# Windowed attention in one core's transformer block: column scores replaced by transposed rows

## The chip, the cores and the metric

The kernel runs on one core of one Trainium2 chip. The metric is the device time of one execution in microseconds (us), the median of several runs. Matrix products run on TensorE (PE in the profile), elementwise work on VectorE (DVE), ScalarE (ACT) and GpSimd (POOL), and SyncE (SP) issues most of the transfers.

## The reference

One block of a hybrid model over 1024 latent and 256 context tokens, width 1024: a combined input projection, a bidirectional scan, windowed attention, merging and output projection, and routed experts. The change concerns attention for the latent queries, with 16 query heads, 4 key and value heads of width 64, blocks of 128 queries, a window of 128 to each side, all 256 context keys, and one sink logit per head in the softmax:

```python
def block(i):
    start = i * ATTN_BLOCK
    qb = lax.dynamic_slice_in_dim(qg, start, ATTN_BLOCK, axis=1)
    kb = lax.dynamic_slice_in_dim(kp, start, span, axis=1)
    ...
    s_loc = jnp.einsum("bqkrd,bskd->bkrqs", qb, kb).astype(jnp.float32)
    s_loc = jnp.where(valid, s_loc, -jnp.inf)
    s_ctx = jnp.einsum("bqkrd,bskd->bkrqs", qb, k_ctx).astype(jnp.float32)
    p = jax.nn.softmax(jnp.concatenate([s_loc, s_ctx, s_sink], -1), axis=-1).astype(v.dtype)
    o = (jnp.einsum("bkrqs,bskd->bqkrd", p[..., :span], vb)
         + jnp.einsum("bkrqs,bskd->bqkrd", p[..., span:-1], v_ctx))
```

All types are float32. The kernel splits queries and keys in a high and a low part for products in the faster fp32r type; the probabilities and values are multiplied in full float32.

## The kernel before

The kernel is a row of stages, each a `Block` in which every engine runs a program of its own and engines wait for each other on semaphores; a stage begins when all engines have left the one before. The order of work on an engine is the order in which the program is written. `scan_output_stage` comes ahead of `attention_stage`; while it runs, SP loads keys, queries and masks of attention into freed buffers (`Early.load`, called with the scan's unit u from 23 on, between the stores of `yT`). Behind it come `branch_stage` and the rest.

`attention_stage` goes over 8 blocks of 128 queries. For a block it scores twice. The row scores (`row_scores`, L1727 and L1728) have queries on the partitions and 640 keys in the columns: `q1` holds a query's high part in rows 0 to 63 and its low part in rows 64 to 127, `k1` the high part of the keys twice, and `k2` the low part of the keys. DVE adds a mask and takes the row maximum (`maximum`, L1839). The maxima of 16 heads, with the sink, are turned (`turn_top`), split in two parts and loaded as two more rows of `q2`, against which `k2` holds ones: so the column scores (`column_scores`, L1743 and L1744), with 128 keys on the partitions and 4 heads x 128 queries in the columns, come out less their maximum. There are 5 key tiles and 4 groups of heads to a block, 4 tiles in the first and last block, 152 tiles in all. DVE masks the two edge tiles (L1857), ACT takes the exponential into `prob` (L1793), and PE sums values with it (`sum_values`, L1755) into `c_ps`: the weights are 64 columns of values, a column of ones, whose row gives the sum of the probabilities, and what follows. ACT copies the sums to `cols` (L1800).

The inverse of the sums takes a way through DRAM: SP gathers the row of sums (L1677), DVE adds the sink's share and inverts (L1866), SP writes the inverses to `inv_rows` and reads them back spread over 64 partitions, DVE divides (L1871), and SP stores the block to `aF` (L1692). `HEADS_AT` lays the row scores and maxima of block m between the column tiles of block m - 1; those of block 0 run alone at the start:

```python
for T in range(LAST):
    column_scores(T)
    if T in TURNS_AT:
        turn_top(TURNS_AT[T])
    if T in HEADS_AT:
        row_scores(*HEADS_AT[T])
    ...
    if T >= LAG:
        sum_values(T - LAG)
```

At the stage's end ACT and DVE also scale the first two tiles of `yT` for the next stage (L1823, L1906), whose first work on PE are the transposes of L2162.

## Time and profile before

| | |
|---|---|
| median of 3 runs | 2686.13 us (2683.49 to 2687.87) |
| span of the profiled execution | 2681.0 us; its own time is not given |
| mean granted clock of PE in it | 0.943 |
| busy, whole span | PE 2448.7 us (91%), DVE 1710.4 (64%), ACT 1090.6 (41%), POOL 466.5 (17%) |
| attention stage | 1226.6 us to 1549.4 us of the span |

The profile is of one execution. Its span runs from the first to the last instruction. Busy times of an engine overlap those of the others; of PE, printed durations contain the pipeline behind a product, so that products that follow each other overlap. The granted clock is a share of 2.4 GHz: 1.00 is the upper level and 0.50, 1.2 GHz, the lower.

### The profile page before, as it was taken

To read this page: it belongs to the slowest core of one execution; us is meant where nothing else is said; L and a number is where in the kernel's file an instruction comes from. 1 tells how busy PE (TensorE), PEld (TensorE's weight loads), DVE (VectorE), ACT (ScalarE), POOL (GpSimd) and SP (SyncE) were. 2 spreads that over 40 slices of the span, in tenths; PEclk is the share of its full clock that TensorE was granted. 3 is DMA by queue.
4 is the path that set the end of the run, shared out by engine and by line. 5 is a ranking of instruction groups with operands and counts; after the bars stand their busy time and mean duration, and the time that the engine had idled before them with its cause. 6 is when DMAs were issued, how large, how long until landed. Compare 5 with 4: busy or idle time off the path is not lost. (4 is left out here: it accounts for less than half of the span.)

```text
span 2681.0 us, 32789 instructions
## 1 busy us (share of the span) xinstructions
PE 2448.7 (91%) x12804; PEld 1996.5 (74%) x12804; DVE 1710.4 (64%) x1828; ACT 1090.6 (41%) x1363; POOL 466.5 (17%) x378
## 2 busy tenths in 40 slices
PE   7899999999999997998999879998982999999993
PEld 2788888887798785666666579997761788888882
DVE  5555555544245764685665467664665799999996
ACT  3333332221131112452333444433331677777772
POOL 0000010021003423792000000001433011111112
PEclk8899999999999998896999979998985999999996
DMA  5222234776337867996335199987335799999994
GB/s 221 77 78 80 74 116 119 184 242 222 109 115 262 300 219 215 315 277 151 62 77 111 41 258 257 255 229 231 117 110 221 296 383 403 403 398 395 396 376 141
DMA packets 359955, 572.12 MB, mean 213 GB/s; under 512 B 24973, under 2 KB 269165, under 8 KB 336449
## 3 DMA queue, kind: packets, MB, share of 16 engines
q1 hardware_dynamic: 328226, 464.99, 52.1%
q0 software_dynamic: 23376, 97.36, 11.3%
q10 hardware_dynamic: 8216, 7.90, 1.2%
q8 instruction: 90, 1.47, 0.2%
q14 instruction: 47, 0.39, 0.0%
HBM read 460.19 MB, written 104.49 MB: 211 GB/s over the span
## 5 line engine op out<-in xcount | busy, mean ns | idle before, releaser
L2714 DVE TENSOR_TENSOR e_wlo<-e_w,e_whi 128x2048 fp32r<-128x2048 f32 x188 | 425.6, 2289 | 43.9 <-ACT e_whi L2663 42.6
L2663 ACT CAST e_whi<-e_w 128x2048 fp32r<-128x2048 f32 x192 | 365.3, 1909 | 125.3 <-PE e_gu L2840 84.1
L460 PE MATMUL f_lat<-h_hi,w_hi 128*128 128x512 f32 x800 | 253.9, 399 | 8.0 <-DVE w_lo L611 8.0
L460 PE MATMUL f_lat<-h_lo,w_hi 128*128 128x512 f32 x800 | 251.2, 395 | 0.0
L460 PE MATMUL f_lat<-h_hi,w_lo 128*128 128x512 f32 x800 | 251.1, 395 | 0.0
L2174 PE MATMUL b_acc<-b_hi,b_whi 128*128 128x256 f32 x768 | 219.0, 285 | 8.3 <-issue 8.3
L2174 PE MATMUL b_acc<-b_lo,b_whi 128*128 128x256 f32 x768 | 218.3, 284 | 0.0
L2174 PE MATMUL b_acc<-b_hi,b_wlo 128*128 128x256 f32 x768 | 218.3, 284 | 0.0
L611 DVE TENSOR_TENSOR w_lo<-w_raw,w_hi 128x1024 fp32r<-128x1024 f32 x50 | 61.2, 1225 | 171.7 <-ACT w_hi L530 171.7
L460 PEld LDWEIGHTS f_lat<-h_hi,w_hi 128*128 128x128 f32 x800 | 137.9, 189 | 38.2 <-DVE w_lo L611 8.6
L1839 DVE CUSTOM_DVE_ANT_0 a_a_ps<-a_a_ps,shared 128x640 f32<-128x640 f32 x128 | 106.5, 833 | 87.6 <-PE a_a_ps L1728 83.0
L460 PEld LDWEIGHTS f_lat<-h_hi,w_lo 128*128 128x128 f32 x800 | 140.1, 188 | 29.8
L460 PEld LDWEIGHTS f_lat<-h_lo,w_hi 128*128 128x128 f32 x800 | 140.0, 188 | 29.8
L1755 PE MATMUL a_c_ps<-a_prob,a_v 128*128 128x512 f32 x304 | 155.8, 595 | 0.0
L2174 PEld LDWEIGHTS b_acc<-b_hi,b_whi 128*128 128x128 f32 x768 | 148.5, 193 | 8.5 <-issue 8.5
L1793 ACT ACTIVATE a_prob<-a_b_ps 128x512 f32<-128x512 f32 x152 | 89.3, 597 | 154.7 <-DVE a_b_ps L1857 88.5
L2174 PEld LDWEIGHTS b_acc<-b_lo,b_whi 128*128 128x128 f32 x768 | 148.5, 193 | 0.0
L2174 PEld LDWEIGHTS b_acc<-b_hi,b_wlo 128*128 128x128 f32 x768 | 148.4, 193 | 0.0
L625 DVE SCALAR_TENSOR_TENSOR conv_acc<-conv_in,conv_tap_cols,conv_acc 128x1284 f32<-128x1284 f32 (+1 forms) x96 | 145.0, 1511 | 3.4
L2840 PE MATMUL e_gu<-e_whi,e_xhi 128*128 128x512 f32 x512 | 140.7, 397 | 3.9 <-DVE e_xlo L2718 2.4
L2840 PE MATMUL e_gu<-e_wlo,e_xhi 128*128 128x512 f32 x512 | 138.6, 393 | 0.0
L2840 PE MATMUL e_gu<-e_whi,e_xlo 128*128 128x512 f32 x512 | 138.6, 393 | 0.0
(374 smaller groups left out, 5434.5 us busy)
## 6 DMA issues: line engine op xcount, KB each, us to landing
e_w<-in_w_gate_up SPq DMA_DIRECT2D x128, 1024.0 KB, 10.8
e_w<-in_w_down SPq DMA_DIRECT2D x64, 1024.0 KB, 9.4
w_raw<-in_w_in SPq DMA_DIRECT2D x50, 512.0 KB, 4.0
t_space<-xbcT POOLq DMA_DIRECT2D x18, 1280.0 KB, 6.4
before<-t_space SPq DMA_DIRECT2D x16, 1024.0 KB, 4.5
shared<-before SPq DMA_DIRECT2D x64, 256.0 KB, 6.2
l_w<-in_w_ssd_br SPq DMA_DIRECT2D x20, 768.0 KB, 6.9
xbcT<-t_out POOLq DMA_DIRECT2D x20, 640.0 KB, 4.4
```

Of the source, the lines that this page charges most:

```text
L460: mm = nc.tensor.matmul(o, weights[:, b, k, :], part[:, k, a:a + n], start=(k == 0 and n_pass == 0), stop=(k == KT - 1 and n_pass == 2))
L611: nc.vector.tensor_tensor(wlo[:, b], w[:, b], whi[:, b].bitcast(F32), ALU.subtract).then_inc(w_free, 1)
L625: nc.vector.scalar_tensor_tensor(conv[:, b, a:W_OUT], padded[:, b, a + c:c + W_OUT], tap[:, b, c:c + 1], conv[:, b, a:W_OUT], ALU.mult, AL ...
L1755: nc.tensor.matmul(out, values(v, c, g), prob[:, T % PR], start=first, stop=last).then_inc(tiles_summed, 1)
L1793: nc.scalar.activation(prob[:, T % PR], b_ps[:, T % 2], ACT.Exp, scale=SCALE).then_inc(exps_made, 1)
L1839: V.tensor_tensor_reduce(a_ps[:, h % 2, A0:A0 + KEYS], a_ps[:, h % 2, A0:A0 + KEYS], mask[variant(m)], 1.0, NEG, ALU.add, ALU.max, top[:, ...
L2174: mm = nc.tensor.matmul(acc[:, b, int(k >= KY), 0:NW], weights[:, b, k, :], part[:, k, at:at + NW], start=(k in (0, KY) and n_pass == 0), ...
L2663: nc.scalar.copy(whi[:, slot % SPLIT], w[:, slot]).then_inc(w_hi, 1)
L2714: V.tensor_tensor(wlo[:, slot % SPLIT], w[:, slot], whi[:, slot % SPLIT].bitcast(F32), ALU.subtract).then_inc(w_split, 1)
L2840: mm = nc.tensor.matmul(gu[:, 512 * c:512 * c + 512], part[:, b, k, :], weights[:, slot % SPLIT, 512 * c:512 * c + 512], start=(k == 0 and ...
```

## The change

Attention scores once. For a pair of heads, PE makes the row scores; the low part of the keys now stands in both halves of `k2`, and the second products of an even and an odd head use rows 0 to 63 and 64 to 127 of the array. The queries lie with their high part in the lower rows for even heads and in the upper for odd ones, so that a block loads in four DMAs; four query buffers replace three pairs. DVE adds the mask and takes the maximum as before, but writes the masked scores to `rows` in SBUF. ACT takes the exponential there with the negative maximum as its bias, and sums the row in the same instruction. PE transposes the probabilities, four heads of a key tile into one tile of `t_ps`, and ACT and DVE copy them in turn to `prob`, which now lies in a part of `l_wo` that the scan uses for its outputs: so ACT and DVE wait at the start until all of `yT` is stored. The value sums of four heads are two matmuls, of 64 weight columns and 256 columns each, into partitions 0 to 63 and 64 to 127. The inverses stay on the chip: POOL multiplies the unit matrix by them, and a product with ones spreads them over the partitions (L1695); DVE multiplies the sums by that. The stores go by half blocks, in four DMAs each. `STEPS` sets the order by hand: a step is a pair of heads, with transposes three steps and value sums five steps behind. Masked keys outside the sequence are left out in blocks 0 and 7, which have 512 keys.

```diff
+        self.spare = flat[:, 2 * D_INNER:4 * D_INNER]
...
-        self.q1 = [queries(one + NK), queries(three), queries(three + 2 * NQ)]
-        self.q2 = [queries(two + NK), queries(three + NQ), queries(three + 3 * NQ)]
+        self.q = [queries(one + NK), queries(two + NK)] + [queries(three + j * NQ) for j in range(2)]
...
+    def load_query(self, eng, qkH, qkL, m):
+        at, j = KV_LAT0 + m * P, m % len(self.q)
+        for half in range(2):
+            for odd in range(2):
+                part = qkH if half == odd else qkL
+                src = part[0:QH * HD, :].rearrange("(h o d) t -> o d h t", o=2, d=HD)[odd, :, :, at:at + P]
+                eng.dma_start(self.q[j][half * HD:half * HD + HD, odd::2].bitcast(F32), src).then_inc(self.q_in[j], 16)
...
-            eng.dma_start(self.k2[HD:HD + 2].bitcast(F32).rearrange("p g t -> p (g t)"), s.flat[1:2, :].to_broadcast([2, KVH * KV_TOK])).then_inc(self.keys_in, 16)
+            self.load_key(eng, qkL, high, self.k2, self.keys_in)
         if u == 29:
-            self.load_query(eng, qkH, low, self.q2[0], 0)
-            self.blank(s, eng, 0)
+            self.load_query(eng, qkH, qkL, 1)
...
-    ORDER = (0, 2, 1, 4, 3)
...
+    RB, TB, VB = 10, 3, 8
...
+    STEPS, BATCHES, MAKER = [], [], []
+    for i in range(STEP_COUNT):
+        step = []
+        u = (i - 3) // 2
+        if 0 <= u < LCHUNK * KVH:
+            half = (FIRST[u + 1] - FIRST[u] + 1) // 2
+            step += [("keys", p) for p in (range(FIRST[u], FIRST[u] + half) if i % 2 else range(FIRST[u] + half, FIRST[u + 1]))]
+        MAKER += [j % 2 for j in range(len(step))]
+        if i >= 7 and i % 4 == 3:
+            step.append(("values", (i - 7) // 4))
+            MAKER.append(0)
+        STEPS.append(range(len(BATCHES), len(BATCHES) + len(step)))
+        BATCHES += step
...
-        prob = own(st, nc, "a_prob", [P, PR, PER_KV, P])
...
+        rows = own(st, nc, "a_rows", [P, RB, KEYS])
+        prob = later.spare.rearrange("p (b h q) -> p b h q", h=PER_KV, q=P)
+        cols = own(st, nc, "a_cols", [P, 2, 2, 2, P])
+        diagonal, ones = own(st, nc, "a_diagonal", [P, 2, PER_KV, P]), own(st, nc, "a_ones", [P, HD])
...
+                def scores(i):
+                    n, g, h = i // HALF, (i % HALF) // 2, (2 * i) % QH
+                    if h == 0:
+                        pe.wait_ge(q_in[n % len(q)], 64 * (n // len(q)) + 64)
+                    a, w = CTX + n * P + (P if n == 0 else 0), width(n) - CTX
+                    spans = ((slice(A0, A0 + CTX), slice(0, CTX)), (slice(A0 + CTX, A0 + CTX + w), slice(a, a + w)))
+                    for odd in range(2):
+                        if i:
+                            pe.wait_ge(maxed, 2 * i - 1 + odd)
+                        for out, keys in spans:
+                            nc.tensor.matmul(a_ps[:, odd, out], q[n % len(q)][:, h + odd], k1[:, g, keys], start=True, stop=False)
+                    for out, keys in spans:
+                        for odd in range(2):
+                            part = slice(HD * odd, HD * odd + HD)
+                            mm = nc.tensor.matmul(a_ps[:, odd, out], q[n % len(q)][part, h + odd], k2[part, g, keys], start=False, stop=True)
+                            if out.start != A0:
+                                mm.then_inc(scored, 1)
...
+                    if kind == "keys":
+                        u, a, _ = PARTS[p]
+                        pe.wait_ge(exps_made, PER_KV * u + PER_KV)
+                        for j in range(PER_KV):
+                            mm = nc.tensor.transpose(out[:, j], rows[:, (PER_KV * u + j) % RB, a:a + P], ident)
+                    else:
+                        pe.wait_ge(diagonal_made, 2 * p + 2)
+                        for a in range(2):
+                            mm = nc.tensor.matmul(out[HD * a:HD * a + HD], ones[:], diagonal[:, a], start=True, stop=True)
+                    mm.then_inc(turned, 1)
...
+                def sum_values(u):
+                    c, g = u // 2, u % KVH
+                    if c >= 1 and u % 2 == 0:
+                        pe.wait_ge(normed, c)
+                    for p in range(FIRST[u], FIRST[u + 1]):
+                        wait_moved(pe, AT[p])
+                        _, _, chunk = PARTS[p]
+                        chunk -= chunk > CCHUNK
+                        for a in range(2):
+                            mm = nc.tensor.matmul(o_ps[HD * a:HD * a + HD, u % 2], v[:, chunk, HD * g:HD * g + HD], prob[:, p % VB, 2 * a:2 * a + 2],
+                                                  start=p == FIRST[u], stop=p + 1 == FIRST[u + 1])
+                        mm.then_inc(valued, 1)
...
+                for i in range(STEP_COUNT):
+                    if i < PAIRS:
+                        scores(i)
+                    if i >= 5 and i % 2 == 1:
+                        if i == 5:
+                            pe.wait_ge(v_in, 32)
+                        sum_values((i - 5) // 2)
+                    for k in STEPS[i]:
+                        turn(k)
...
+                def exponential(h):
+                    w = width(h // QH)
+                    act.wait_ge(negated, h // 2 + 2)
+                    nc.scalar.activation(rows[:, h % RB, 0:w], rows[:, h % RB, 0:w], ACT.Exp, scale=SCALE, bias=negtop[:, h:h + 1],
+                                         accum_out=sums[:, h:h + 1]).then_inc(exps_made, 1)
...
+                for g in range(GROUPS):
+                    act.wait_ge(later.y_out[g], 16 * LCHUNK)
+                    act.sem_inc(act_carrier, 1)
...
+                    V.tensor_tensor_reduce(rows[:, h % RB, 0:w], a_ps[:, h % 2, A0:A0 + w], mask[variant(n)][:, 0:w], 1.0, NEG,
+                                           ALU.add, ALU.max, top[:, h:h + 1]).then_inc(maxed, 1)
...
+                    V.tensor_tensor(cols[:, c % 2], o_ps[:], cols[:, c % 2], ALU.mult).then_inc(normed, 1)
...
+                for i in range(STEP_COUNT):
+                    if i < PAIRS:
+                        maximum(2 * i)
+                        maximum(2 * i + 1)
+                        negate(i)
+                        if i % 4 == 3:
+                            sink_argument(i // 4)
+                    if i >= 5 and i % 4 == 1:
+                        invert((i - 5) // 4)
+                    if i >= 8 and i % 4 == 0:
+                        norm((i - 8) // 4)
+                    for k in STEPS[i]:
+                        if MAKER[k] == 1:
+                            move(k)
...
+                        share = inverse[:, HALF * c + PER_KV * a:HALF * c + PER_KV * a + PER_KV]
+                        nc.gpsimd.tensor_tensor(diagonal[:, a], ident.unsqueeze(1).to_broadcast([P, PER_KV, P]),
+                                                share.unsqueeze(2).to_broadcast([P, PER_KV, P]), ALU.mult).then_inc(diagonal_made, 1)
...
```

On PE, before, an inner block repeats these rows (`a_c_ps` value sums, `a_b_ps` column scores, `a_a_ps` row scores of one head); each row of a value sum is two records in the trace.

```order
L1755 MATMUL a_c_ps<-a_prob,a_v 128x512
L1743 MATMUL a_b_ps<-shared 128x512
L1744 MATMUL a_b_ps<-shared 128x512
L1727 MATMUL a_a_ps<-shared 128x256
L1728 MATMUL a_a_ps<-shared 128x256
L1727 MATMUL a_a_ps<-shared 128x384
L1728 MATMUL a_a_ps<-shared 128x384
```

On PE, in the change, an odd step with the spreading of inverses and the even step behind it, in an inner block (`a_o_ps` value sums, `a_t_ps` transposes and spread inverses):

```order
L1678 MATMUL a_a_ps<-shared 128x256 x2
L1678 MATMUL a_a_ps<-shared 128x384 x2
L1707 MATMUL a_o_ps<-l_wo,a_v 64x256 x10
L1691 MATMUL a_t_ps<-shared,a_rows 128x128 x12
L1695 MATMUL a_t_ps<-a_diagonal,a_ones 64x512 x2
L1674 MATMUL a_a_ps<-shared 128x256
L1674 MATMUL a_a_ps<-shared 128x384
L1674 MATMUL a_a_ps<-shared 128x256
L1674 MATMUL a_a_ps<-shared 128x384
L1678 MATMUL a_a_ps<-shared 128x256 x2
L1678 MATMUL a_a_ps<-shared 128x384 x2
L1691 MATMUL a_t_ps<-shared,a_rows 128x128 x8
```

The column scores have gone, and the value sums of a group, spread over five tiles before, stand in one piece ahead of twelve transposes.

On SP's queue, at the end of the scan stage, the rows of the change from unit 27 on:

```order
L1211 DMA shared<-qkL 64x4x1536
L1332 DMA yT<-l_wo 128x512
L1211 DMA shared<-qkL 64x4x1536
L1332 DMA yT<-l_wo 128x512
L1219 DMA shared<-qkH 64x8x128
L1219 DMA shared<-qkL 64x8x128 x2
L1219 DMA shared<-qkH 64x8x128
L1332 DMA yT<-l_wo 128x512
L1240 DMA shared<-const_masks 128x640
L1332 DMA yT<-l_wo 128x512
```

Before, the second load of `qkL` was one of 2x6144 constants, and the four loads of queries were one of 64x16x128 and one of 2x2048 constants.

## Rows read from the trace of the kernel before

**Rows 1.** Busy time by stretch, attention stage; columns named in the first row.
```profile
core 0: us, PE busy (x) PEld busy (x) DVE busy (x) ACT busy (x) POOL busy (x), PEclk, DMA share, GB/s
1226.00:1257.00 31.00, 26.82 (x86) 20.31 (x87) 18.32 (x43) 3.16 (x3) 0.00 (x0) 0.50 0.84 165
1257.00:1536.00 279.00, 271.31 (x1044) 180.46 (x1042) 156.61 (x328) 109.71 (x198) 4.27 (x6) 0.99 0.34 70
1536.00:1549.00 13.00, 0.00 (x0) 0.00 (x0) 6.12 (x12) 5.85 (x8) 0.00 (x0) 0.57 0.20 49
```

**Rows 2.** Order of time (start, duration, engine, line, operation, idle before), PE, first products.
```profile
1226.59 0.55 PE L1727 MATMUL a_a_ps<-shared 128*128 128x256 f32 x1 [8.87 <-DMA shared<-const_flat]
...
1549.44 0.45 PE L2162 MATMUL b_tp<-l_ident,l_wo 128*128 128x128 f32 x1 [13.69 <-PEq L1635]
```

**Rows 3.** Order of time, PE and DVE, a step within block 3.
```profile
1411.72 0.28 PE L1727 MATMUL a_a_ps<-shared 128*128 128x256 f32 x1
...
1411.84 0.28 PE L1728 MATMUL a_a_ps<-shared 66*128 66x256 f32 x1
...
1411.96 0.34 PE L1727 MATMUL a_a_ps<-shared 128*128 128x384 f32 x1
...
1412.14 0.34 PE L1728 MATMUL a_a_ps<-shared 66*128 66x384 f32 x1
...
1412.31 1.02 PE L1755 MATMUL a_c_ps<-a_prob,a_v 128*128 128x512 f32 x2
1412.69 0.83 DVE L1839 CUSTOM_DVE_ANT_0 a_a_ps<-a_a_ps,shared 128x640 f32<-128x640 f32 x1 [1.03 <-PE a_a_ps L1728]
...
1413.40 0.40 PE L1744 MATMUL a_b_ps<-shared 66*128 66x512 f32 x1
...
1413.44 0.14 DVE L1839 DVE_READ_ACCUMULATOR2_ANT a_top<- 128x1 f32 x1
1413.64 0.28 PE L1727 MATMUL a_a_ps<-shared 128*128 128x256 f32 x1
```

**Rows 4.** Order of time, SP's queue, the store of a block's sums.
```profile
1532.27 0.63 SPq L1692 DMA_DIRECT2D aF<-a_cols  x1
```

**Rows 5.** Order of time, PE, eight transposes in the projection stage.
```profile
109.77 1.04 PE L479 MATMUL f_tp<-squares,f_out 128*128 128x128 f32 x8
```

**Rows 6.** Groups by line, DVE and ACT: shapes, count, busy us, mean ns.
```profile
L1857 DVE TENSOR_TENSOR a_b_ps<-a_b_ps,shared 128x512 f32<-128x512 f32 x56 | 39.0, 696 | 27.6 <-PE a_b_ps L1744 27.6
...
L1800 ACT COPY a_cols<-a_c_ps 128x512 f32<-128x512 f32 x32 | 18.8, 586 | 21.8 <-PE a_c_ps L1755 21.7
...
L1009 ACT ACTIVATE t_space<-t_space 128x640 f32<-128x640 f32 x1 | 0.7, 738 | 0.0
...
L1823 ACT ACTIVATION_READ_ACCUMULATOR a_a_ps<-l_wo 128x1 f32 x2 | 0.4, 190 | 0.0
```

**Rows 7.** Busy time by stretch, scan stage; columns as in group 1.
```profile
1160.00:1180.00 20.00, 19.70 (x105) 13.79 (x103) 15.58 (x31) 11.44 (x40) 18.64 (x17) 1.00 0.88 300
1190.00:1226.00 36.00, 27.27 (x144) 19.03 (x142) 23.79 (x39) 16.07 (x58) 31.56 (x25) 0.92 1.04 240
```

**Rows 8.** Order of time, the scan's last store and the first maximum.
```profile
1221.91 0.32 SPq L1333 DMA_DIRECT2D yT<-l_wo  x1
...
1228.17 0.83 DVE L1839 CUSTOM_DVE_ANT_0 a_a_ps<-a_a_ps,shared 128x640 f32<-128x640 f32 x1 [6.36 <-PE a_a_ps L1728]
```

**Rows 9.** Order of time, ACT and DVE, the end of attention.
```profile
1536.27 1.89 ACT L1823 ACTIVATE a_a_ps<-l_wo 128x2048 f32<-128x2048 f32 x1
...
1538.29 1.28 ACT L1825 ACT_TABLE_LOAD   x1
1538.30 0.15 DVE L1900 TENSOR_SCALAR l_mean<-l_ssq 128x1 f32<-128x1 f32 x1 [6.12 <-ACT a_a_ps L1823]
...
1539.82 1.28 DVE L1906 TENSOR_SCALAR l_wo<-l_wo,l_root 128x2048 f32<-128x2048 f32 x1 [0.69 <-ACT l_root L1825]
...
1545.39 2.49 DVE L1871 TENSOR_TENSOR a_cols<-a_cols,a_inverse 64x512 f32<-64x512 f32 x4 [1.78 <-DMA a_inverse<-inv_rows]
```

More of the change, by code:

```diff
@@ L1574, in attention_stage, with tiles @@
-    FIRST = [TILES.index((n, 0, 0)) for n in range(LCHUNK)]
-    LAST = len(TILES)
-    ENDS = [T for T in range(LAST) if T + 1 == LAST or TILES[T + 1][1] != TILES[T][1]]
-    LAG = 3
-    PR, QB = 6, 3
-    A0 = 256
-    LEAD = 3
-    VW = HD + 2
-    INVERT, DIVIDE = 8, 12
+    STEP_COUNT = PAIRS + 4
+    def tiles(n):
+        first = 1 if n == 0 else 0
+        last = 2 if n == LCHUNK - 1 else 3
+        return [(P * t, t) for t in range(CCHUNK)] + [(CTX + P * (t - first), CCHUNK + n + t) for t in range(first, last)]
@@ new lines, in width @@
+    def width(n):
+        return P * len(tiles(n))
+    PARTS = [(u, a, v) for u in range(LCHUNK * KVH) for a, v in tiles(u // KVH)]
+    FIRST = [[p for p, part in enumerate(PARTS) if part[0] == u][0] for u in range(LCHUNK * KVH)] + [len(PARTS)]
+    STEPS, BATCHES, MAKER = [], [], []
[11 more added lines that the diff above has]
+        BATCHES += step
@@ L1583, in attention_stage @@
+    RANK = [MAKER[0:k + 1].count(MAKER[k]) for k in range(len(BATCHES))]
+    AT = [BATCHES.index(("keys", p)) for p in range(len(PARTS))]
     with ExitStack() as st:
-        ident, edge, mask, k1, k2, q1, q2 = early.ident, early.edge, early.mask, early.k1, early.k2, early.q1, early.q2
+        ident, mask, k1, k2, q = early.ident, early.mask, early.k1, early.k2, early.q
         sink, negsink = own(st, nc, "a_sink", [P, QH]), own(st, nc, "a_negsink", [P, QH])
-        v = own(st, nc, "a_v", [P, NV * KVH * VW + P - VW])
@@ L1625, in edges_before, with wait_moved @@
[L1625 to L1644 removed]
+        def wait_moved(eng, k):
+            eng.wait_ge(moved[MAKER[k]], RANK[k])
@@ L1714, in _ @@
+                for c in range(HALVES):
+                    store(c)
+                    m = len(q) + c // 2
+                    if c % 2 == 0 and m < LCHUNK:
+                        sp.wait_ge(scored, QH * (m - len(q) + 1))
+                        early.load_query(sp, qkH, qkL, m)
             @block.tensor
             def _(pe):
-                def row_scores(m, h):
-                    g, j, i = h // PER_KV, m % QB, QH * m + h
+                def scores(i):
+                    n, g, h = i // HALF, (i % HALF) // 2, (2 * i) % QH
@@ L1746, in sum_values @@
-                def sum_values(T):
-                    n, g, t = TILES[T]
-                    group = G * n + g
-                    first, last = T == 0 or T - 1 in ENDS, T in ENDS
-                    if first and group >= 2:
-                        pe.wait_ge(kept, group - 1)
-                    pe.wait_ge(exps_made, T + 1)
-                    c = t if t < CCHUNK else n + t
-                    out = c_ps[:, group % 2]
-                    nc.tensor.matmul(out, values(v, c, g), prob[:, T % PR], start=first, stop=last).then_inc(tiles_summed, 1)
+                        pe.wait_ge(q_in[n % len(q)], 64 * (n // len(q)) + 64)
@@ L1868, in divide @@
-                def divide(n, g):
-                    heads = slice(PER_KV * g, PER_KV * g + PER_KV)
-                    dve.wait_ge(inv_in, 16 * n + 16)
-                    V.tensor_tensor(cols[0:HD, n % 2, heads], cols[0:HD, n % 2, heads], inverse[:, heads], ALU.mult).then_inc(divided, 1)
-                dve.wait_ge(early.const_in, 48)
-                for h in range(QH):
-                    maximum(0, h)
-                dve.wait_ge(const_in, 32)
-                V.tensor_scalar(negsink[:], sink[:], -1.0 / SCALE, None, ALU.mult).then_inc(negated, 1)
@@ L1898, in inverse_mean @@
+                norm(HALVES - 1)
                 def inverse_mean(n):
@@ L2011, in _ @@
                 load_gates(0)
-                sp.wait_ge(later.a_out, 16 * LCHUNK)
+                for out in later.a_out:
+                    sp.wait_ge(out, 64 * LCHUNK)
                 load_piece(2)
```

376 lines of the change are left out of this document (117 added, 259 removed).

## Prediction

> **What bounds the kernel now.** I read the page first, then the busy time by stage, then the order of single instructions inside attention, and last the waits. The attention stage runs from PE's first score product at 1226.6 us to the first product of the next stage at 1549.4 [rows 1, 2]: 322.8 us. The reader should see three stretches in it [rows 1]. Up to 1257 the row scores and maxima of block 0 run alone, with PE at 26.82 busy of 31.00 us and a granted clock of 0.50, the lower level (1.2 GHz). From 1257 to 1536 PE is busy 271.31 of 279.00 us at 0.99, while DVE and ACT have 156.61 and 109.71: PE is the bound. From 1536 to 1549 PE has nothing: the last sums go through DRAM and back, and the next stage waits.
>
> In the middle stretch the starts tell what a product costs PE, as its printed durations overlap [rows 3]. One head of row scores starts products at 1411.72, 1411.84, 1411.96 and 1412.14 and the value sums at 1412.31: 0.12 us for 256 columns, 0.175 for 384, 0.59 a head. From the value sums to the next head it is 1.33 us; the two column score products take 0.235 each (1413.40 to 1413.64), which leaves 0.86 for a value tile. It is two records of 0.43 each in the trace. A block with five key tiles so costs PE 16 x 0.59 + 20 x (0.47 + 0.86) = 36.0 us.
>
> **What PE gives and takes.** The column scores go: 20 x 0.47 = 9.4 us a block, and with them the loading of maxima. The row scores stay. Added are 80 transposes a block; eight of them take 1.04 us, and without the 0.165 of pipeline behind the last (below) 0.11 each [rows 5], 8.8 us. The value tile becomes two matmuls of 256 columns, each with 64 columns of weights, into partitions 0 to 63 and 64 to 127. A pair of heads now has its second score products on rows 0 to 63 and 64 to 127 of the array. Whether such halves run side by side no row of this trace shows, since no two neighbouring products in it use separate parts of the array. The bounds are 0.43 and 0.86 us for a value tile, and 0.295 and 0.59 for the second products of a pair. The nearest row is the upper one. I still take the lower: the halves share no rows or columns of the array, no output partition and no wait, and each pair stands in a row on PE's queue. The products that spread the inverses (two of 512 columns, two halves of 0.43 each) take 1.29, as only the middle of four pieces overlaps; 1.72 without it.
>
> The Trainium skill ("TensorE: Matmul & The Clock Gate", Part 3) says that matmuls in distinct column groups run concurrently, with a measured 2.38x for three. The Trainium skill's "TensorEngine Tiling (Array Packing)", Key Properties, speaks against the change: switching the tiling mode drains TensorE. By the first page the sum is my 2647 below, where the upper row gives the 2740 of the first rival; by the second, the upper bound of the next part holds, 16 us more. No run here shows either yet.
>
> **What a change of shape costs.** A 384-column product is printed with 0.34 us and holds PE for 0.175 [rows 3], so emptying the array is worth at most 0.165; at least nothing. An inner block has 24 changes (5 in a pair of steps, 4 for the inverses): 0 to 4 us, and I take 2.
>
> **One step.** The new loop goes by pairs of heads, and PE's queue is: scores, in odd steps the value sums of a group of four heads, transposes. Scores have two buffers, and their second products end both, so PE and DVE take turns. From a last score product to its maximum it is 0.55 us (1412.14 to 1412.69), from one maximum to the next 0.89 (0.83 and 0.14 with an overlap), from a maximum's start to PE's next product 0.95 (1412.69 to 1413.64) [rows 3]. Even step: 0.55 + 0.89 + 0.95 = 2.39, then the second head's first products 0.295 and one of 0.12: the next last product starts after 2.81 us. Its eight transposes (0.88) lie in the wait. Odd step: 0.17 for the rest of the product, five value tiles 2.15, twelve transposes 1.32, four first products 0.59, and 0.12: 4.35, with the maxima (2.39) hidden. Four such pairs and two inverse products make an inner block 4 x 7.16 + 2.6 + 2 = 33.2 us. In blocks 0 and 7, with four tiles a head, it is 3.3 and 2.5: 4 x 5.8 + 2.6 + 2 = 27.8. Six and two: 254.8 us.
>
> The others fit below that. DVE in an inner block: 16 x 0.89, eight copies out of PSUM (a masked add over the same 128x512 tile takes 0.70 [rows 6]) 5.6, two norms 1.4, and small ones 2.5: 23.7. ACT: sixteen exponentials of 640 columns, 0.74 by the row of that width and 0.19 for the sum [rows 6], and fourteen copies of 0.59 [rows 6]: 23.1. POOL has four products a block, and two steps' time for each two. Were PE half as long, DVE's 23.7 would be the floor.
>
> **Ends.** The first steps have no transposes or sums (-4 us). The last pair's exponentials, transposes, copies and sums run bare: two maxima 1.5, ACT 1.9, sixteen transposes 1.8, copy and wait 0.9, values 1.7, the inverse 1.3 and the norm 0.7, about 10. The clock: PE is idle for 8.9 us before the stage [rows 2] and more now, so it starts at 1.2 GHz. A pair of steps then has about 12 us of PE work for 7.2. The stay there is between none and the 31 us of [rows 1]: 0 to 12 us, and I take 7. From first maximum to last sum: 254.8 - 4 + 10 + 7 = 268.
>
> The start: DVE and ACT now wait until the last yT store has landed, since prob lies in its buffer. SP's queue holds 1.5 MB more ahead of it for the second half of k2, 0.5 for block 1's queries, 0.2 less of masks and edges. The DMA engines are full there at 240 GB/s (1.04 of their time) [rows 7], so the store lands up to 8 us later, and the first maximum starts at 1236.2 instead of 1228.2 [rows 8]; bounds 0 and 12. Stores of a half block are now four DMAs, 64 issues at 0.63 us [rows 4], 40 us of SP's time, hidden.
>
> The tail: PE's 13.7 us wait [rows 2] held the sums' way through DRAM and two squares of 1.9 us [rows 9]. The squares now run beside the last sums. Left are six small instructions of 0.15 to 0.20 us for means and roots, the root's table 1.28, two scalings of 1.28, and the way into the next stage, 1.5 from the end of the last divide (1545.39 and 2.49) to 1549.4 [rows 2, 9]: with hand-overs 6.5.
>
> **The sum.** 1236.2 + 268 + 6.5 = 1510.7, against 1549.4: 38.7 us less. The stages behind it do what they did. The profiled span is 2681.0; its own time is not given, but the median of the three runs, 2686.1, lies 5.1 above, and I count these 5 us as what lies around the span. 2681.0 - 38.7 + 5.1 = **2647 us**.
>
> The bounds of this case: change of shape 0 or 4 a block (-16, +16), clock (-7, +5), start (-8, +4), and the second score products one behind the other (+0.29 in each of 64 steps, +19). Not all at once: **2620 to 2675**.
>
> **The rivals.**
> *The halves of the array don't run side by side*: the change then doesn't do what it says. A value tile stays at 0.86, an odd step is 6.80 and an even one 3.10. An inner block is 4 x 9.9 + 3.4 + 2 = 45.0, an edge block 37.5; with ends of 16 (my 13, and longer last sums) they make 361, and 1236.2 + 361 + 6.5 = 1603.7, 54 more: **2740**. This is the other side; it decides from about 0.68 us a value tile, where the 38.7 are used up (152 tiles x 0.25). For it: no row shows an overlap. Against it: the waits allow it. Chance 0.20.
> *The clock falls in the even steps.* PE idles there twice for about 0.6 us and is otherwise on transposes. For it: from 1226 to 1257 PE was 87% busy and stayed at 0.50 [rows 1]. Against it: in the scan stage before, with short products, it is 98.5% busy and stays at 1.00 [rows 7], and the wait after which the clock was low was longer, 8.9 us [rows 2]. If half the steps run at 1.2 GHz, a block gains 10 us: +80, **2727**. Chance 0.08. "TensorE: Matmul & The Clock Gate", Part 4 of the Trainium skill, says that the full clock doesn't engage for transposes, since they don't count as busy in the same way. By it this rival and its 2727 would be likelier; the transposes at 0.11 us of [rows 5] stand between long products and don't settle it.
> *Values overlap, but the turn-taking costs more*: late copies into three PSUM tiles or late exponentials hold PE, 0.3 us a step and the score halves in a row: +19 + 19, **2685**, no change. Chance 0.06; where only half of it comes, it is about 2666 and within my case.
> My own case has 0.66.
>
> **Chances and range.** A change of 0.2% (5 us) is about what this kernel's runs can tell from none. Faster 0.69 (my case and half of the third rival), within 0.2% 0.03 (its other half), slower 0.28 (the first two). The range reaches from my case's low end to the first rival with little beyond: 2618 to 2742.
>
> **What would show it.** In the profile after: a value tile's two halves at starts that make 0.43 a tile (0.86 is the first rival); even steps near 2.8 us and odd ones near 4.4 from last score product to last; transposes 0.11 apart; granted clock 1.00 after the first 20 us; first maximum near 1236; the next stage's first transposes near 1511, 6 to 7 us after the last value sum. I am wrong if the stage is longer than 323 us, or if DVE, not PE, has no idle time in it.

## The result, and the profile after

| | before | after |
|---|---|---|
| median, same chip | 2686.73 us (4 runs, 2683.49 to 2687.87) | 2637.26 us (4 runs, 2633.18 to 2639.67) |
| ratio | | 0.982, 95% interval 0.980 to 0.983 |
| span of the profiled execution | 2681.0 us | 2637.1 us |
| attention, PE's first product to the next stage's | 322.8 us | 268.3 us |

The change makes the kernel 49 us faster; 2647 had been forecast, with 2620 to 2675 for the likeliest case. In the profile the gain is 44 us. Three marks split it: the scan's last product on DVE, the first maximum, and the first product of the next stage.

Order of time of the kernel after, DVE and PE (start, duration, engine, line, operation, shapes, idle before):

```profile
1226.58 0.69 DVE L1514 TENSOR_TENSOR l_wo<-l_w,l_wo 128x512 f32<-128x512 f32 x1
...
1236.31 1.19 PE L1674 MATMUL a_a_ps<-shared 128*128 128x256 f32 x4 [13.14 <-POOL a_ones L1846]
...
1241.83 0.18 DVE L1807 TENSOR_SCALAR a_negsink<-a_sink 128x16 f32<-128x16 f32 x1 [14.56 <-DMA a_sink<-in_attn_sink]
1242.56 0.69 DVE L1775 CUSTOM_DVE_ANT_0 a_rows<-a_a_ps,shared 128x512 f32<-128x512 f32 x1 [0.55 <-DVE a_negsink L1807]
...
1500.11 0.69 DVE L1800 TENSOR_TENSOR a_cols<-a_o_ps,a_cols 128x512 f32<-128x512 f32 x1 [3.60 <-ACT a_cols L1739]
...
1504.58 3.40 PE L2098 MATMUL b_tp<-l_ident,l_wo 128*128 128x128 f32 x16 [5.13 <-PEq L1635]
```

The same product that ends the scan, before the change:

```profile
1221.12 0.69 DVE L1515 TENSOR_TENSOR l_wo<-l_w,l_wo 128x512 f32<-128x512 f32 x1
```

From the scan's last product to the first maximum it was 7.05 us (1221.12 to 1228.17 [rows 8]) and is 15.98. From the first maximum to the next stage it was 321.3 us ([rows 2, 8]) and is 262.0. So the change gives 59.3 us and takes 8.9 at the start: 50.4 net, where the medians differ by 49.5. The profile shows less because its scan, whose arithmetic is the same, ended 5.5 us later than in the execution of before, and the stages behind took 1 us more. In the twelve further profiles below this product starts anywhere from 1219.6 to 1228.2 us, so nothing about attention is read from it; all intervals below start behind it.

Busy time by stretch, after (columns as in [rows 1]):

```profile
1226.00:1242.00 16.00, 1.92 (x8) 1.43 (x8) 1.41 (x3) 0.00 (x0) 0.15 (x2) 0.55 1.08 255
1242.50:1258.00 15.50, 13.10 (x66) 10.08 (x68) 9.68 (x31) 8.77 (x23) 0.00 (x0) 0.60 1.05 180
1258.00:1499.00 241.00, 234.76 (x1722) 157.76 (x1718) 154.13 (x417) 157.38 (x355) 36.74 (x38) 1.00 0.23 51
```

PE still bounds the stage (234.76 of 241 us), DVE and ACT have 154 and 157, and the clock is at its upper level but for the part up to 1258 (0.55 and 0.60 in the first two rows). The reader should see that "busy" is too kind here: PE's printed products contain their pipeline, and the steps show idle time that this row does not.

Order of time, PE, two steps inside block 3:

```profile
1364.55 0.56 PE L1678 MATMUL a_a_ps<-shared 64*128 64x256 f32 x4
...
1365.04 1.09 PE L1691 MATMUL a_t_ps<-shared,a_rows 128*128 128x128 f32 x8
...
1366.03 0.56 PE L1674 MATMUL a_a_ps<-shared 128*128 128x256 f32 x2
...
1366.77 0.56 PE L1674 MATMUL a_a_ps<-shared 128*128 128x256 f32 x2 [0.18 <-DVE a_top L1775]
...
1367.26 0.56 PE L1678 MATMUL a_a_ps<-shared 64*128 64x256 f32 x4
...
1367.75 2.38 PE L1707 MATMUL a_o_ps<-l_wo,a_v 128*64 128x256 f32 x20
...
1370.07 1.53 PE L1691 MATMUL a_t_ps<-shared,a_rows 128*128 128x128 f32 x12
...
1371.35 0.83 PE L1674 MATMUL a_a_ps<-shared 128*128 128x256 f32 x4
...
1372.11 0.56 PE L1678 MATMUL a_a_ps<-shared 64*128 64x256 f32 x4
```

Five value tiles take 2.32 us from start to start, 0.464 each, against 0.86 before ([rows 3]): the halves run side by side. The single records of this row tell it more closely. Each of the ten products is two records; the two halves' records start 0.007 us apart, and the next two 0.216 behind them. So a tile inside the row costs 0.432 us, and the remaining 0.16 of the 2.32 stand at its two ends, where the shape of the products changes. Twelve transposes take 1.28. The four second products, worth 0.295 us of columns, hold PE for 0.49. In the even step (1364.55 to 1367.26, 2.71 us) the first head's first products start at 1366.03 and are worth 0.295, yet the second head's start at 1366.77, when its maximum has freed the buffer: 0.44 us without work. The odd step (1367.26 to 1372.11) is 4.85 us and has none.

### The profile page after: what moved, and what is told of

It reads as the page before. It is cut to its first block and busy times, and to the rows that moved or that the text cites. A ratio compares the mean times of both kernels' runs of the same rounds, so it can differ in the third digit from the quotient of the medians.

```text
span 2637.1 us, 34496 instructions
## 1 busy us (share of the span) xinstructions
PE 2404.6 (91%) x13468; PEld 1967.1 (75%) x13468; DVE 1696.2 (64%) x1900; ACT 1140.2 (43%) x1538; POOL 497.9 (19%) x410
## 5 line engine op out<-in xcount | busy, mean ns | idle before, releaser
L2845 POOL DMA_INDIRECT moe<-e_y,e_token x15 | 42.2, 2811 | 498.3 <-DVE e_y L2671 468.0
L1775 DVE CUSTOM_DVE_ANT_0 a_rows<-a_a_ps,shared 128x640 f32<-128x640 f32 (+1 forms) x128 | 96.0, 788 | 48.2 <-PE a_a_ps L1678 47.6
L1729 ACT ACTIVATE a_rows<-a_rows,a_negtop 128x640 f32<-128x640 f32 (+1 forms) x128 | 101.6, 796 | 31.1 <-DVE a_negtop L1781 31.0
```

The source lines that it names most:

```text
L1729: nc.scalar.activation(rows[:, h % RB, 0:w], rows[:, h % RB, 0:w], ACT.Exp, scale=SCALE, bias=negtop[:, h:h + 1], accum_out=sums[:, h:h + ...
L1775: V.tensor_tensor_reduce(rows[:, h % RB, 0:w], a_ps[:, h % 2, A0:A0 + w], mask[variant(n)][:, 0:w], 1.0, NEG, ALU.add, ALU.max, top[:, h:h ...
L2845: pool.indirect_dma_start(moe, bass.IndirectOffsetOnAxis(ap=token[:, e:e + 1], axis=0), y[:, e % 2], None, compute_op=ALU.add).then_inc(y_ ...
```

## The experiments

Each kernel is the change with one edit, or an earlier one of these with one more. They ran on several chips, each beside runs of the kernel before on its own chip, whose medians go from 2683.8 to 2687.2: the ratios, not the medians, compare kernels of different chips. Beside medians I use two intervals of each profile: A, from the scan's last product to the first maximum, and B, from the first maximum to the start of DVE's last multiplication of the sums. Kernels with the same start differ in A by 1 us (e4 and e7 by 1.7), and kernels with the same steps in B by 0.3, so B tells far more than a median, whose runs spread over 3 to 11 us.

| kernel | median us | ratio to before (95%) | A us | B us |
|---|---|---|---|---|
| the change | 2637.3 | 0.982 (0.980 to 0.983) | 16.0 | 257.6 |
| e1 value halves apart | 2678.7 | 0.996 (0.994 to 0.997) | 17.0 | 297.2 |
| e2 full rows | 2635.9 | 0.981 (0.979 to 0.983) | 16.3 | 257.2 |
| e3 by head | 2615.0 | 0.973 (0.972 to 0.975) | 16.5 | 237.6 |
| e4 start | 2629.6 | 0.979 (0.977 to 0.980) | 11.4 | 257.4 |
| e5 by head, 64 rows | 2666.7 | 0.993 (0.990 to 0.996) | 16.3 | 285.2 |
| e6 double transposes | 2681.5 | 0.999 (0.998 to 1.000) | 16.4 | 304.3 |
| e7 = e3 + e4 | 2611.7 | 0.973 (0.971 to 0.976) | 9.7 | 237.4 |
| e8 = e7, later waits | 2609.4 | 0.972 (0.970 to 0.975) | 7.6 | 237.5 |
| e9 = e8, shorter tail | 2607.0 | 0.971 (0.969 to 0.972) | 7.8 | 237.0 |
| e10 = e9, sums split | 2615.5 | 0.973 (0.972 to 0.975) | 7.8 | 244.1 |
| e11 sums split alone | 2620.3 | 0.975 (0.973 to 0.977) | 16.4 | 243.1 |
| e12 = e9, stores shared | 2606.4 | 0.970 (0.968 to 0.971) | 7.5 | 237.1 |

### Do the halves run side by side?

**e1.** The loops over tiles and halves change places.

```diff
-                    for p in range(FIRST[u], FIRST[u + 1]):
...
-                        for a in range(2):
+                    for a in range(2):
+                        for p in range(FIRST[u], FIRST[u + 1]):
...
```

> Same products in another order: the five products into partitions 0 to 63 first, then the five into 64 to 127, so that neighbours use the same columns of the array. Theory A (the halves of a value tile run side by side and PE bounds the odd steps): a tile goes from the 0.464 us read after the change (five in 2.32) towards 0.86; with the one overlap left between the two rows of five that is 4 x 0.4 = 1.6 to 1.9 us a group, 32 groups, +51 to +61 us: 2688 to 2698. Theory B (the gain came from the dropped column scores and the way through DRAM, and an odd step has slack or the overlap is not what makes the tile short): under +15 us, 2637 to 2652, and the value sums still take about 2.3 us a group.

Order of time, PE, e1:

```profile
1365.60 3.72 PE L1707 MATMUL a_o_ps<-l_wo,a_v 128*64 128x256 f32 x20
...
1369.25 0.98 PE L1691 MATMUL a_t_ps<-shared,a_rows 128*128 128x128 f32 x7
```

The same ten products take 3.65 us instead of 2.32, B grows by 39.6 us and the median by 41: theory A in kind, less in size. The reason is in the records. Below are stretches of 0.43 us within the value sums, PE busy and PEld busy as in [rows 1], where x counts the records in progress. The first is of the change; the other two are of e1, early in its row and in its middle:

```profile
1368.71:1369.14 0.43, 0.43 (x8) 0.29 (x6) 1.00 0.54 118
```

```profile
1366.48:1366.91 0.43, 0.43 (x3) 0.27 (x2) 1.00 0.36 81
1367.34:1367.77 0.43, 0.43 (x7) 0.33 (x4) 1.00 0.71 151
```

In e1 the ten records of one half go at 0.216 us a record, so a tile one half after the other costs 0.86 us, as before the change. But the other half's records begin 0.64 us before the first half's last one starts, and all 24 groups of five tiles look alike: there the halves overlap again. I had allowed for one overlapping product of 0.43. With none, e1 would be longer by 0.75 us in each of 32 groups and the loss about 64 us, an estimate from these starts (152 tiles of 0.43 are 65). So side by side is worth 0.43 us a tile, and without it the change's gain is gone.

### What is a change of shape worth?

**e2.** The second products use all rows:

```diff
-                            mm = nc.tensor.matmul(a_ps[:, odd, out], q[n % len(q)][part, h + odd], k2[part, g, keys], start=False, stop=True)
+                            mm = nc.tensor.matmul(a_ps[:, odd, out], q[n % len(q)][:, h + odd], k2[:, g, keys], start=False, stop=True)
```

> The second score products use all 128 rows (the low part of the keys lies in both halves, so this adds the product of the low parts) and can't run side by side; the array keeps one shape from scores to transposes. Theory A (side by side is worth 0.295 us a step and a change of shape next to nothing): +0.295 x 64 = +19 us, 2656. Theory B (the four second products take 0.49 us of which only 0.295 is columns, so a change of shape costs about 0.2 us, and with a second one before the transposes the packing of rows earns nothing): 0.59 for 0.49, and about 0.1 less in the transposes: -3 to +6 us, 2634 to 2643.

**e3** does the same and finishes each head before the next:

```diff
                         for out, keys in spans:
                             nc.tensor.matmul(a_ps[:, odd, out], q[n % len(q)][:, h + odd], k1[:, g, keys], start=True, stop=False)
-                    for out, keys in spans:
-                        for odd in range(2):
...
+                        for out, keys in spans:
+                            mm = nc.tensor.matmul(a_ps[:, odd, out], q[n % len(q)][:, h + odd], k2[:, g, keys], start=False, stop=True)
+                        mm.then_inc(scored, 1)
```

> As the full-row kernel, but each head is finished before the next one starts, so that its maximum can begin about 0.5 us earlier. Theory A (the 0.44 us that PE waits in each even step is turn-taking with DVE over two score buffers): that wait shrinks by 0.3 to 0.44 us in 32 even steps, 10 to 14 us less than the full-row kernel, about 2628. Theory B (DVE's and ACT's own work, or the copies, set the even step): the same as the full-row kernel within 3 us.

**e5** is e3 with the second products on `part`, the 64 rows of the change.

> Head by head as in the third run, but with the second products on 64 rows, as in the change: nothing runs side by side, and the products go 128, 64, 128, 64 rows in every step. Against the third run (2615) only the shape changes, four in a step where there were none. Theory A (a change of shape empties the array; the full-row kernel showed 0.49 for columns worth 0.295 on the way in and about 0.09 less in the transposes behind, so about 0.3 us for in and out): +0.5 us in each of 64 steps on a PE without idle time, +25 to +37 us, 2640 to 2652. Theory B (a change of shape costs nothing by itself): 2612 to 2618.

e2 costs nothing against the change (B 257.2 and 257.6): theory B. In the change the second products of a pair do start together, 0.003 us apart, so the overlap is there and something else takes its worth. PE in e2, the same two kinds of rows:

```profile
1364.10 0.83 PE L1674 MATMUL a_a_ps<-shared 128*128 128x256 f32 x4
1364.77 0.75 PE L1677 MATMUL a_a_ps<-shared 128*128 128x256 f32 x4
1365.37 0.38 PE L1690 MATMUL a_t_ps<-shared,a_rows 128*128 128x128 f32 x2
```

First and second products take 0.67 and 0.60 here, 1.27; in the change 0.76 and 0.50 (1371.35 to 1372.11 to 1372.61), 1.26. Products that overlap in pairs but change the shape twice cost what products in a row cost that don't. (Behind the scores of an odd step stand value sums, whose shape is another in both kernels. So e2 drops three changes in a pair of steps, 0.57 us at the price below, for 0.59 us of columns.)

e5 against e3 tells the price itself, since nothing runs side by side in either. PE in e5, then in e3, one step of scores each:

```profile
1368.97 0.54 PE L1674 MATMUL a_a_ps<-shared 128*128 128x256 f32 x2
1369.44 0.56 PE L1677 MATMUL a_a_ps<-shared 64*128 64x256 f32 x2
1369.93 0.56 PE L1674 MATMUL a_a_ps<-shared 128*128 128x256 f32 x2
1370.42 0.55 PE L1677 MATMUL a_a_ps<-shared 64*128 64x256 f32 x2
1370.90 1.09 PE L1689 MATMUL a_t_ps<-shared,a_rows 128*128 128x128 f32 x8
```

```profile
1369.59 0.54 PE L1674 MATMUL a_a_ps<-shared 128*128 128x256 f32 x2
1369.96 0.46 PE L1676 MATMUL a_a_ps<-shared 128*128 128x256 f32 x2
1370.26 0.45 PE L1674 MATMUL a_a_ps<-shared 128*128 128x256 f32 x2
1370.55 0.46 PE L1676 MATMUL a_a_ps<-shared 128*128 128x256 f32 x2
1370.85 1.03 PE L1688 MATMUL a_t_ps<-shared,a_rows 128*128 128x128 f32 x8
```

Each pair of products takes 0.49 us with a change of shape behind it and 0.295 without: 0.19 to 0.20 us a change. B grows by 47.6 us. Four changes in an even step and three in an odd one (its fourth was there in e3, ahead of the value sums) are 224 in all, 0.21 each; the median grows by 52. Both are more than theory A's 25 to 37, which had put in and out together at 0.3.

### Is the even step's idle time turn-taking?

e3 answered it too: 21 us less than e2, where 10 to 14 had been expected, and 19.6 in B. In its inner steps the rows of PE show no wait; a pair of steps without inverses takes 7.00 us (transposes at 1363.85 and again at 1370.85) against 7.57 in the change. e2 and e3 have the same rows and shapes, so all of the 19.6 us is the order's; the waits for a maximum account for 12 of them (below), and what the other 7 are is open. Against the change e3 holds two edits, so **e11** takes the idle time alone. It is the change, with two of the five value tiles moved into the even step.

```diff
+                    half = (FIRST[u] + FIRST[u + 1] + 1) // 2
...
-                    for p in range(FIRST[u], FIRST[u + 1]):
+                    for p in range(half, FIRST[u + 1]) if second else range(FIRST[u], half):
...
-                    if i >= 5 and i % 2 == 1:
+                    if i >= 5:
...
-                        sum_values((i - 5) // 2)
+                        sum_values((i - 5) // 2, i % 2 == 0)
```

> The change itself, with the value sums in two parts as in the tenth kernel and nothing else. Theory A (in the change the even step is set by the turns of PE and DVE over two score buffers, with 0.44 us of PE idle): sums moved there fill the idle time; 14 us less, 3 to 6 back for the added passages, 2626 to 2629. Theory B (the gain of the head-by-head order came from something else, such as the dropped shape changes): no gain, 2637 or more.

2620.3 us and B 14.4 us less: theory A, and the passages cost nothing that shows. PE waits for `a_top` for 12.3 us in the change; in e11 that wait is not among its first seven. Waits from 1258 to 1499 of the change, then to 1485 of e11 (us in total, times, longest):

```profile
PEld a_a_ps L1674 <- DVE a_top L1775: 12.3, 29, 0.4
```

```profile
ACT l_wo L1741 <- PE a_t_ps L1691: 61.4, 84, 1.4
DVE a_rows L1777 <- PE a_a_ps L1678: 43.4, 47, 2.0
PEld a_t_ps L1691 <- issue: 22.7, 59, 0.4
```

**e10** makes the same split on top of e9, which has the order of e3 and so no idle time left to fill.

> The ninth kernel, with the value sums of a group in two parts, three tiles in the odd step and two in the even one. Theory A (with the head-by-head order PE has no idle time left in the even steps, so that balancing them only adds passages between scores, sums and transposes, about 0.1 us in 32 steps): +3 us against the ninth. Theory B (PE still waits for maxima or copies, some 20 us in small pieces): 5 to 10 us less than the ninth.

B grows by 7.1 us and the median by 8.5: there the split only costs, over twice what I expected, and e10 ends where e11 does (244.1 and 243.1). The two ways to fill the idle time don't add up. Why the split costs 7 us there is not shown.

### Does the clock mind the transposes?

**e6** makes every transpose twice.

> Every transpose of the change is made twice into the same place. Theory A (transposes cost 0.11 us each at the full clock, PE bounds the step except for 0.44 us in each even one): 608 more at 0.11 are 67 us, less 32 x 0.44 = 14 hidden: about +53 us, 2690, and the granted clock stays at 1.00. Theory B (the clock falls where transposes make up more of PE's work): the clock in the stage is below 0.95 and the time is over 2720. Theory C (PE has slack): under +15 us.

+44 us in the median (45 by the ratios), +46.7 in B, where 53 was expected. Busy time of e6:

```profile
1258.00:1540.00 282.00, 282.00 (x2270) 217.32 (x2270) 153.99 (x409) 157.09 (x350) 34.75 (x36) 1.00 0.19 43
```

The clock stays at 1.00 with 1216 transposes in the stage, so theory B falls, and as the time grows by nearly all of the added work, C does too: outside the even step PE has no slack. The Trainium skill ("TensorE: Matmul & The Clock Gate", Part 4) says that the full clock doesn't engage for transposes. In this mix, where they stand between products on a PE that is never idle for long, it does.

### What holds the start?

**e4** moves two loads behind the last store of `yT`.

```diff
-        if u == 29:
-            self.load_query(eng, qkH, qkL, 1)
-        if u == 30:
-            eng.dma_start(self.mask[1], s.masks[1]).then_inc(self.mask_in, 16)
...
+                early.load_query(sp, qkH, qkL, 1)
+                sp.dma_start(mask[1], s.masks[1]).then_inc(early.mask_in, 16)
                 early.load_query(sp, qkH, qkL, 2)
```

> The queries of block 1 and the middle mask (0.8 MB) are issued behind the last store of yT. Theory A (SP's queue holds back the store, for which ACT, DVE and all of the stage wait): the store before the last no longer waits 9.6 us for four query DMAs, the first maximum starts 6 to 10 us earlier, and the time is 2627 to 2631. Theory B (the DMA engines are full anyway, or the scan's own arithmetic ends that late; or block 1's queries then come late): the first maximum moves by under 3 us, 2634 to 2640, or PE waits for the queries of block 1.

SP's queue in the change, then in e4 (a row of several DMAs goes from the first one's start to the last one's end; the three stores of e4 take 0.32 us each, between waits for their data):

```profile
1220.80 0.32 SPq L1332 DMA_DIRECT2D yT<-l_wo  x1
1221.17 0.58 SPq L1219 DMA_DIRECT2D shared<-qkH  x1
1221.79 7.59 SPq L1219 DMA_DIRECT2D shared<-qkL  x2
1229.42 1.25 SPq L1219 DMA_DIRECT2D shared<-qkH  x1
1230.78 3.75 SPq L1332 DMA_DIRECT2D yT<-l_wo  x1
1234.57 0.43 SPq L1240 DMA_DIRECT2D shared<-const_masks  x1
1235.12 0.38 SPq L1332 DMA_DIRECT2D yT<-l_wo  x1
```

```profile
1214.86 6.89 SPq L1328 DMA_DIRECT2D yT<-l_wo  x3
1222.14 0.33 SPq L1645 DMA_DIRECT2D a_sink<-in_attn_sink  x1
```

The queries' four DMAs hold SP for 9.5 us, 6.9 of them one DMA, two stores wait behind them, and SP, with them every engine, leaves the stage that late. With the loads behind the stores A falls by 4.6 us; the median falls by 7.6. Theory A in kind; the trace gives less than its 6 to 10.

What holds the first maximum in e4 is another wait, DVE's for the sink's load, which SP issued at 1222.14:

```profile
1231.29 0.17 DVE L1805 TENSOR_SCALAR a_negsink<-a_sink 128x16 f32<-128x16 f32 x1 [9.95 <-DMA a_sink<-in_attn_sink]
1232.01 0.69 DVE L1773 CUSTOM_DVE_ANT_0 a_rows<-a_a_ps,shared 128x512 f32<-128x512 f32 x1 [0.55 <-DVE a_negsink L1805]
```

The last store of `yT`, issued 0.7 us ahead of it, lands 0.2 us earlier. With the DMA engines full both take 9 to 10 us to land, and in the change 6 to 6.5.

**e7** has both edits.

> The head-by-head order of the third run and the later loads of the fourth together. If the two gains lie in different places they add up: 22 us and 7.6 us off the changed kernel, 2607. If the earlier start only meets PE's own work or block 1's queries come late: 2612 to 2616.

**e8** also loads the last 768 columns of `k2` behind the stores, takes the sink over ACT's queue, and lets ACT and DVE wait for the outputs only in step 3, ahead of their first copy into `prob`:

```diff
-                for g in range(GROUPS):
-                    act.wait_ge(later.y_out[g], 16 * LCHUNK)
-                    act.sem_inc(act_carrier, 1)
+                act.dma_start(sink[:], s.x["attn_sink"].to_broadcast([P, QH])).then_inc(sink_in, 16)
                 for i in range(STEP_COUNT):
+                    if i == 3:
+                        for g in range(GROUPS):
+                            act.wait_ge(later.y_out[g], 16 * LCHUNK)
+                            act.sem_inc(act_carrier, 1)
```

> As the seventh run, and further: the last 640 keys of both halves of k2 (1.25 MB) are loaded behind the last store, the sink comes over ACT's queue, and ACT and DVE wait for the landed outputs only ahead of their first copy into prob. Theory A (the start waits for bytes queued ahead of it): PE's first product and the first maximum come 4 to 6 us earlier, about 2602. Theory B (the scan's own last sums and the stage's hand-over set the start): within 2 us of the seventh run.

e7 came to 2611.7, at the edge of its second expectation, and e8 to 2609.4, nearer its theory B. Here too DVE waits for the sink:

```profile
1232.91 0.17 DVE L1808 TENSOR_SCALAR a_negsink<-a_sink 128x16 f32<-128x16 f32 x1 [6.67 <-DMA a_sink<-in_attn_sink]
```

The stores have landed at 1228.7 and PE's first products are done by 1229.5, but the sink, issued on ACT's queue at 1227.06, lands at 1232.9. So in e8, and in e9, e10 and e12 with the same start, a load of 8 KB holds the first maximum; no run here issues it earlier.

In the traces the parts add up: A goes 16.5, 9.7, 7.6 from e3 to e7 to e8, and B stays. In the times little of it shows: the ratio moves from 0.973 to 0.972. The intervals of ±0.002 to 0.003 (4 to 7 us) don't decide it: the ratios of e3 and e8 differ by 2 us, their A by 9, and what the start is worth in the time stays open between these.

### What holds the end?

**e9** takes squares, means, roots and scalings off the end: the squares in eight pieces of 512 columns in steps 48 to 55 of ACT.

> The eighth kernel, with the work for the next stage taken off the end of attention: the two squares of 2048 columns become eight of 512 in steps 48 to 55 of ACT, means and roots come before the last exponentials' copies, and DVE scales the two tiles in its idle time of the last steps. Theory A (the last sum to the next stage, 4.5 us, is this work, and one square delays a last copy by about 1.1 us): about 4 us less, 2605. Theory B (ACT has no room for 8 x 0.8 us in the steps, or the last copies wait for PE anyway): 2608 to 2611.

Order of time, end of e9:

```profile
1464.98 0.69 DVE L1804 TENSOR_TENSOR a_cols<-a_o_ps,a_cols 128x512 f32<-128x512 f32 x1 [1.04 <-ACT a_cols L1739]
1465.76 2.53 SPq L1645 DMA_DIRECT2D aF<-a_cols  x4
1468.92 1.00 SPq L1953 DMA_DIRECT2D l_wo<-aF  x2
...
1469.13 3.38 PE L2109 MATMUL b_tp<-l_ident,l_wo 128*128 128x128 f32 x16 [4.81 <-PEq L1633]
```

A miss by the intervals; the medians (2609.4 and 2607.0, on two chips) can't tell. B is 0.5 us shorter and the way from the last multiplication to the next stage 4.15 us for 4.46: 0.8 of the expected 4. What had been late next is seen in the rows: SP issues the four stores of the last half block for 2.53 us, and the stage ends with it. **e12** lets ACT issue two of them.

> The ninth kernel, with the last half block's four stores issued by SP and ACT, two each. In the ninth the next stage starts 4.15 us after the last multiplication of the sums starts, and SP issues four stores of 0.63 us in between. Theory A (the end of SP's issues opens the next stage): 1.3 us earlier, 2.9 us between the two, too little for the median to show: 2602 to 2607. Theory B (the stage's hand-over or another engine sets it): 4.1 us as before.

The way shrinks to 3.15 us (1466.47 to 1469.62), 1.0 of the expected 1.3. That confirms the cause for this part of the tail; the median (2606.4) can't show it. e12 has the lowest ratio of these kernels, 0.970, 31 us below the change, though 2606.4 and e9's 2607.0 can't be told apart.

## Why the prediction was right

**The value tile, 0.43.** Measured 0.432 inside a row and 0.464 with the row's two ends, and by e1 it is the overlap that makes it. The term carried the forecast and was right. It was a bet against the nearest row of the trace, with no run behind it. The Trainium skill's rule that matmuls in distinct column groups run concurrently ("TensorE: Matmul & The Clock Gate", Part 3) holds for two halves of 256 columns, with 0.86 to 0.43 us a tile. The first rival, that the halves don't run side by side, was wrong. Its price of 93 us is not refuted by e1's 41, since e1 keeps part of the value overlap, the second score products in pairs and the inverses as they were; for the value sums alone the rival's 0.43 a tile is what the records give.

**The second score products, 0.295, and 0 to 4 us a block for changes of shape.** Here two terms stood side by side that are one. The columns take 0.295, but each of the two changes around them costs 0.19 us or more (e5), above the 0.165 that I had allowed as the most: that bound was mis-sized. Two of them in each of eight steps are 3.0 us a block, where I had taken 2 for all 24 changes; so packing the rows gains nothing (e2). The rule that I cited against the change (the Trainium skill, "TensorEngine Tiling (Array Packing)", Key Properties: switching the mode drains TensorE) agrees with this trace in that every change of shape costs time.

**The steps.** Even 2.71 for 2.81, odd 4.85 for 4.35: the odd one lacked two changes of 0.19 and, at the ends of the value sums, 0.17. The inverse product took 1.01 for 1.29 (1362.76 to 1363.77): all of its pieces overlap. The maxima of 640 columns start in 1268.45 and those of 512 again in 1462.97, six inner blocks, 32.4 us each for 33.2: a pair of steps took 7.57 for 7.16, but the 2 us for changes had been counted apart, and the inverses 0.6 too high.

**Ends and clock, -4 + 10 + 7.** The two outer blocks with all ends took 63.7 us (258.2 less 194.5), where 55.6 + 13 had been forecast: 5 too much. The clock was at 0.60 for 15.5 us, within the bounds. That steps which take turns with DVE lose little by a slow PE, and that this is where the 5 us went, is argued only.

**The start, +8.** 8.9 by interval A. The forecast named the last store, landing late behind the bytes of the new loads. It does land late, at 1241.6, and the sink's load at 1241.8; but both are issued late, at 1235.12 and 1235.89, behind the four DMAs of queries. The forecast had no term for SP's issues being held, and that its 8 us came out is in part luck. **The tail, 6.5** from the end of the last multiplication, was 3.8.

**The other rivals.** The clock did not fall (e6 too). The third one, costlier turns, put 0.3 us a step on late copies; the wait of 0.44 us in even steps was in my own 2.81 already, as part of the turn. What I did not ask is whether this turn had to be: e3 and e11 each take it away, in two different ways.

**The sum.** 38.7 forecast, 50.4 by the intervals, 49.5 by the medians: 5 from ends and clock, 5 from the inner blocks, 3 from the tail, 1 back at the start. Within an inner block the errors partly cancelled: its four pairs of steps came out 1.6 us longer than summed, against the 2 us set apart for changes of shape and 0.6 too much for the inverses.

## What to carry to other kernels

Products that use separate halves of the array pay where they stand in long rows of one shape: ten value products of 0.43 us took 2.32 us in pairs, while four score products between others gained nothing, for each change of shape cost 0.19 us. The order within the row counts: with all of one half ahead of the other (e1) the same ten took 3.65 us. Where PE and DVE take turns over two buffers, finish one buffer before filling the next; a share of busy time of 97% hid 12 us of such waits. When a load is moved into the queue that also carries a stage's last store, its time of issue counts against the next stage. Four loads of queries in pieces of 512 bytes held SP for 9.5 us here, where loads of keys in pieces of 6144 bytes, just ahead, took 0.58 each (1212.26 and 1216.16); whether it is the size of the pieces or what is queued by then no run separates. And issue early even the smallest load that a stage's first instructions need: here 8 KB took 6 to 9 us to land while the other loads went on.

## What was not expected of the hardware

- A change between 128 and 64 rows costs 0.19 us. It is seen in the distances between starts, about half ahead of the new shape's first product and half behind it; the printed durations (0.46 and 0.56) show half of it.
- Full-precision products of 256 columns with 64 columns of weights take 0.43 us one after the other, and 0.43 for two side by side.
- Four DMAs of 64 x 8 x 128 elements hold SP's queue for 9.5 us when the DMA engines are full (1221.17 to 1230.67, DMA at 1.03 of its time), and for 3 us otherwise (1370.18 to 1373.41, DMA at 0.58).
